# Router fed with unnormalised residual rows, the expert choice taken in two parts, the first-block token table built without counts, and the overflow table moved into the expert turns

## What is computed

```python
h = x + m @ w_out
# channel mixer
xn = rmsnorm(h, norm2_g)
lg = xn @ w_group_router + b_group_router               # 4 groups
grp = argmax(lg); p_grp = softmax(lg)[grp]
le = (xn @ w_expert_router + b_expert_router)[grp]      # 8 experts of that group
top_v, top_i = top_k(le, 2)
wt = p_grp * softmax(top_v); eid = grp * 8 + top_i      # 2 of 32 experts for each row
y = sum over the row's two experts of wt * ((silu(xn @ w_gate[e]) * (xn @ w_up[e])) @ w_down[e])
out = h + y
```

## Time and profile before

| | |
|---|---|
| median of 3 runs | 1861.66 us (1856.81 to 1862.01) |
| the profiled execution's own time | 1863.4 us |
| its span | 1861.6 us |
| PE, DVE, ACT, POOL busy | 93%, 54%, 42%, 17% of the span |
| chain that ended last, by engine | PE 91%, DVE 3%, DMA 3%, ACT 1% |
| TensorE clock granted, mean | 0.96 of full speed |

### The profile page before, as it was taken

One profiled execution on the slowest core, in us unless ns is written; L12 is line 12 of the kernel. 1 busy time (PEld: TensorE's weight loads), 2 busy tenths in 40 slices (PEclk: granted clock), 3 DMA queues, 4 the chain that ended last, 5 costly groups with the idle time before them and its releaser, 6 DMA issues.

```text
span 1861.6 us, 28131 instructions
## 1 busy us (share of the span) xinstructions
PE 1737.7 (93%) x11006; PEld 1560.7 (84%) x11014; DVE 1004.9 (54%) x1392; ACT 774.0 (42%) x1038; POOL 314.6 (17%) x344
## 2 busy tenths in 40 slices
PE   6999999999989999999999899659999999999980
PEld 5999988899979999888899788648888888888870
DVE  5104211277743333212365433359998988989964
ACT  5222211133332223222311222227787878878860
POOL 0001200000101113010101400013333332333310
PEclk9999999999989989999999999769999999999995
DMA  5322432221223223443664322339999999999957
GB/s 183 125 90 83 148 122 78 74 91 64 96 87 110 83 79 109 131 145 118 195 215 129 98 97 87 153 132 379 378 382 380 387 392 392 392 383 383 390 203 292
DMA packets 122881, 365.55 MB, mean 196 GB/s; under 512 B 19089, under 2 KB 79057, under 8 KB 96578
## 3 DMA queue, kind: packets, MB, share of 16 engines
q1 hardware_dynamic: 102210, 312.76, 46.2%
q0 software_dynamic: 19344, 46.99, 6.9%
q10 hardware_dynamic: 1232, 4.46, 0.6%
HBM read 330.41 MB, written 68.52 MB: 214 GB/s over the span
## 4 chain that ended last, share of the span: by engine, by line
PE 91%; DVE 3%; DMA 3%; ACT 1%; issue 1%; POOL 0%; SPq 0%; DVEq 0%; POOLq 0%; ACTq 0%
PE ps L791 15%; PE ps L792 15%; PE ps L793 15%; PE ps L1173 6%; PE ps L1175 6%; PE ps L1174 6%; PE ps L1196 3%; PE ps L1197 3%; PE ps L1198 3%; PE ps L1029 2%; PE ps L966 2%; PE ps L940 2%; PE ps L1162 2%; DMA out_y_prompt<-part 1%; PE ps L1031 1%; PE ps L950 1%
## 5 line engine op out<-in xcount | busy, mean ns | idle before, releaser
L791 PE MATMUL ps<-part,part 128*128 128x256 f32 (+3 forms) x1912 | 609.9, 319 | 11.3 <-DVE part L1783 6.9
L792 PE MATMUL ps<-part,part 128*128 128x256 f32 (+3 forms) x1912 | 595.8, 312 | 0.0
L793 PE MATMUL ps<-part,part 128*128 128x256 f32 (+3 forms) x1912 | 595.6, 311 | 0.0
L1899 DVE TENSOR_TENSOR part<-part,part 128x2048 fp32r<-128x2048 f32 x192 | 440.0, 2293 | 62.0 <-ACT part L1456 57.8
L1456 ACT ACTIVATE part<-part 128x2048 fp32r<-128x2048 f32 x192 | 368.2, 1919 | 116.8 <-PE ps L1175 82.9
L791 PEld LDWEIGHTS ps<-part,part 128*128 128x128 f32 x1912 | 368.2, 193 | 20.1 <-DVE part L1783 8.3
L792 PEld LDWEIGHTS ps<-part,part 128*128 128x128 f32 x1912 | 368.6, 193 | 4.8
L793 PEld LDWEIGHTS ps<-part,part 128*128 128x128 f32 x1912 | 367.7, 192 | 5.1
L1173 PE MATMUL ps<-part,part 128*128 128x512 f32 x512 | 203.8, 398 | 3.5 <-DVE part L1949 3.5
L1175 PE MATMUL ps<-part,part 128*128 128x512 f32 x512 | 200.8, 392 | 0.0
L1174 PE MATMUL ps<-part,part 128*128 128x512 f32 x512 | 200.3, 391 | 0.0
(11 more groups left out here) (229 smaller groups left out, 2017.3 us busy)
## 6 DMA issues: line engine op xcount, KB each, us to landing
part<-w_gate SPq DMA_DIRECT2D x64, 1024.0 KB, 7.8
part<-w_up SPq DMA_DIRECT2D x64, 1024.0 KB, 7.4
part<-w_down SPq DMA_DIRECT2D x64, 1024.0 KB, 7.2
part<-w_in SPq DMA_DIRECT2D x25, 1024.0 KB, 5.4
part<-x_prompt SPq DMA_DIRECT2D x16, 512.0 KB, 3.6
part<-expert_out_scratch SPq DMA_DIRECT2D x8, 1024.0 KB, 6.7
gate_scratch<-part POOLq DMA_DIRECT2D x32, 192.0 KB, 3.0
part<-gate_scratch SPq DMA_DIRECT2D x4, 1088.0 KB, 6.3
```

The lines of the kernel that those rows point to most:

```text
L791: mm(out, lhs[0](k), rhs[0](k), start=(k == 0), stop=False)
L792: mm(out, lhs[0](k), rhs[1](k), start=False, stop=False)
L793: last = mm(out, lhs[1](k), rhs[0](k), start=False, stop=(k == n - 1))
L1899: tt(elo[:, off % NSPL, :], eraw[:, off % NRAW, :], ehi[:, off % NSPL, :].bitcast(F32), ALU.subtract)\
```

## The change

Four things change, and nothing of the expert turns' own work.

1. PE transposes `hbuf`, the rows before normalisation, instead of `x2`. `norm2_g` is multiplied into the router's weights once (`wr` by `g2T`, a sixth load of the router's group, in which each partition gets eight single elements), and the row's reciprocal root is multiplied in when the logits are taken. PE's transposes of a tile stand between the halves of the next tile's matmuls, and its router follows that tile: both one tile sooner than before. On ACT, for the last tile alone, the copy of the transposed rows comes ahead of the root.
2. The choice is made for the first seven tiles of `TORD` (`NEARLY`) ahead of the last tile's sum, and for the other two after the last logits. Ranks count in the order `TORD`.
3. The first-block table needs no counts: the row in the block is the rank itself (a rank of 128 or more matches nothing), the column is the expert. POOL's first three gathers take their indices straight from `tabt`.
4. Counts, overflow bases, slots and the overflow table are made in pieces between expert turns: on PE after turns 2, 4 and 12, on DVE after turns 1, 3 to 11 and 14. The turns up to there are written out, PE's from 2 to 12 and DVE's from 1 to 14. The tokens' weights `wts` (after turn 1) are one of the pieces. `table_ready` 1 is the first-block table, 2 the overflow table, for which only the code after the last turn waits.

```diff
@@ pe @@
-        def x2_transposes(t):
-            pe.wait_ge(s("x2_ready"), t + 1)
+        def h_transposes(i):
+            pe.wait_ge(s("h_ready"), i + 1)
+            if i >= 1:
+                pe.wait_ge(s("hT_ready"), i)
             for k in range(KT):
-                last = tr(pair(4)[:, k, :], x2[t % 2][:, P * k:P * k + P], ident)
+                last = tr(pair(4)[:, k, :], hbuf[:, TORD[i], P * k:P * k + P], ident)
...
+            if i >= 1:
+                out_half(i, 0)
+                h_transposes(i - 1)
+                last = out_half(i, 1)
             last.then_inc(s("out_mm"), 1)
-            if t >= 1:
-                x2_transposes(t - 1)
-            if t >= 2:
-                router(t - 2)
-        router(TILES - 2)
-        x2_transposes(TILES - 1)
+            if i >= 1:
+                router(i - 1)
+        pe.wait_ge(s("assign"), 1)
+        ranks(0, NEARLY)
+        h_transposes(TILES - 1)
         router(TILES - 1)
...
+        pe.wait_ge(s("onehot"), 1)
+        table(0, NEARLY)
+        pe.wait_ge(s("assign"), 2)
+        ranks(NEARLY, TILES)
+        pe.wait_ge(s("onehot"), 2)
+        table(NEARLY, TILES).then_inc(s("tab_mm"), 1)
...
+        OVER_PE = {2: count, 4: block_base, 12: over_table}
...
-        with pe.Fori(2, NE - 1) as b:
+        for b in range(2, 13):
+            gate_up(b, loop_chunks(b), b)
+            x_tr(b + 1)
+            down(b - 1, loop_chunks(b), b)
+            h_tr(b)
+            if b in OVER_PE:
+                OVER_PE[b]()
+        with pe.Fori(13, NE - 1) as b:
@@ dve @@
-            tt(lgt[:, TORD[t], :], bank(6, RW), rbias, ALU.add).then_inc(s("route_in"), 1)
+            stt(lgt[:, i, :], bank(6, RW), small[:, 2, i:i + 1], rbias, ALU.mult, ALU.add).then_inc(s("route_in"), 1)
...
+        def one_hot(t0, t1, part):
+            n = t1 - t0
+            dve.wait_ge(s("rank_mm"), part)
+            ranks = ps[:, 7, NE * t0:NE * t1].rearrange("p (t e) -> p t e", e=NE)
+            for j in range(2):
+                own.done(tt(prank[:, 2 * t0 + j:2 * t1:2, :], E12[:, t0:t1, j, :], ranks, ALU.mult))
+            dve.wait_ge(s("dve_own"), own.n)
+            step(v.tensor_reduce(R["sl"][:, t0:t1, :].rearrange("p t j -> p (t j)"), prank[:, 2 * t0:2 * t1, :], AX.X, ALU.add))
+            tt(in_row[:, 2 * t0:2 * t1, :], cst[:, CIOTA:CIOTA + P].unsqueeze(1).to_broadcast([P, 2 * n, P]),
+               R["sl"][:, t0:t1, :].rearrange("p t j -> p (t j)").unsqueeze(2).to_broadcast([P, 2 * n, P]), ALU.is_equal)\
+                .then_inc(s("onehot"), 1)
...
-        dve.wait_ge(s("rout_in"), 80)
+        dve.wait_ge(s("rout_in"), 96)
+        tt(wr, wr, g2T.unsqueeze(2).to_broadcast([P, KT, RW]), ALU.mult).then_inc(s("wr_ready"), 1)
...
+            if t == TILES - 1:
+                one_hot(0, NEARLY, 1)
...
+            if t == NEARLY:
+                select(0, NEARLY)
+        logits(TILES - 1)
+        select(NEARLY, TILES)
+        one_hot(NEARLY, TILES, 2)
+        dve.wait_ge(s("tab_mm"), 1)
+        step(tsc(tabs[:, 0:NE], ps[:, 2, 0:NE], float(EMPTY), None, ALU.add))
+        tsc(tabt[:, 0:NE], tabs[:, 0:NE], 1, None, ALU.logical_shift_right).then_inc(s("table_ready"), 1)
...
+        OVER_DVE = {1: weights, 3: over_count, 4: over_rank, 5: over_base, 6: over_pos, 7: over_slot, 8: over_where,
+                    9: lambda: over_onehot(0), 10: lambda: (over_onehot(1), over_column()), 11: over_experts, 14: over_tables}
...
-        with dve.Fori(1, NE - 1) as b:
+        for b in range(1, 15):
+            turn(b)
+            if b in OVER_DVE:
+                OVER_DVE[b]()
+        with dve.Fori(15, NE - 1) as b:
             turn(b)
@@ pool @@
-        gather(0, 0)
-        for b in range(1, 3):
-            pool.wait_ge(s("xg_tr"), b)
-            gather(b, b)
+        for b in range(3):
+            if b > 0:
+                pool.wait_ge(s("xg_tr"), b)
+            pool.indirect_dma_start(xg, None, xn_d, bass.IndirectOffsetOnAxis(ap=tabt[:, b:b + 1], axis=0),
+                                    bounds_check=T - 1, oob_is_err=False).then_inc(s("xg_in"), 16)
```

More of the change, by code:

```diff
@@ L100, in constants @@
     c[:, CVALID:CVALID + TILES] = 1
-    c[NSAMP:, CVALID + ST] = 0
+    c[NSAMP:, CVALID + TORD.index(ST)] = 0
     c[:, CEPS] = EPS
@@ L294, in _build @@
     g2b = lh.take(D)
+    g2T = lh.take(KT)
     lh2 = Lay(2 * KT * T + WSLOT)
@@ L298, in _build @@
     x2 = [lh2.take(D) for _ in range(2)]
-    x2T = [lh2.take(KT, P) for _ in range(2)]
+    hTr = [lh2.take(KT, P) for _ in range(2)]
     assert lh2.at <= AFTER_W
@@ L1109, in router, with out_half @@
+        def router(i):
+            pe.wait_ge(s("hT_ready"), i + 1)
+            if i == 0:
+                pe.wait_ge(s("wr_ready"), 1)
+            if i >= 1:
+                pe.wait_ge(s("route_in"), i)
             for k in range(KT):
-                last = mm(bank(6, RW), x2T[t % 2][:, k, :], wr[:, k, :], start=(k == 0), stop=(k == KT - 1))
+                last = mm(bank(6, RW), hTr[i % 2][:, k, :], wr[:, k, :], start=(k == 0), stop=(k == KT - 1))
             last.then_inc(s("rout_mm"), 1)
-        for t in range(TILES):
-            pe.wait_ge(s("m_split"), t + 1)
-            if t >= 2:
-                pe.wait_ge(s("h_ready"), t - 1)
-            if t == 0:
+        def out_half(i, half):
+            return three(bank(2 * (i % 2) + half), [lambda k, v=v: v[i % 2][:, k, :] for v in (mh, ml)],
+                         [lambda k, v=v: v[:, k, 512 * half:512 * half + 512] for v in wo], KT)
@@ new lines, in _, with ranks, table @@
+        ones, before_row = cbf[:, BONE:BONE + P], cbf[:, BLT:BLT + P]
+        def ranks(first, end):
+            for i in range(first, end):
+                out = ps[:, 7, NE * i:NE * i + NE]
+                for i2 in range(i):
+                    mm(out, ones, Abf[:, i2, :], start=(i2 == 0), stop=False)
+                last = mm(out, before_row, Abf[:, i, :], start=(i == 0), stop=True)
+            last.then_inc(s("rank_mm"), 1)
+        def table(first, end):
+            for n in range(2 * first, 2 * end):
+                last = mm(ps[:, 2, 0:NE], in_row[:, n, :], num_col[:, n, :], start=(n == 0), stop=(n == 2 * TILES - 1))
+            return last
@@ L1118, in _ @@
+        for i in range(TILES):
+            pe.wait_ge(s("m_split"), i + 1)
+            if i >= 2:
+                pe.wait_ge(s("h_ready"), i - 1)
+            if i == 0:
                 pe.wait_ge(s("b_gated"), NB_U)
-            for j in range(4 if t == 0 else 0):
+            for j in range(4 if i == 0 else 0):
                 pe.wait_ge(s("w_split"), WO + 1 + j)
@@ L1129, in _ @@
-            if t >= 2:
-                router(t - 2)
-        router(TILES - 2)
-        x2_transposes(TILES - 1)
-        router(TILES - 1)
-        pe.wait_ge(s("assign"), 1)
-        pe.wait_ge(s("route_in"), TILES)
-        ones = cbf[:, BONE:BONE + P]
-        for t in range(TILES):
-            out = ps[:, 0, NE * t:NE * t + NE]
-            order = [ST] + list(range(NTILE))
-            before = order[:order.index(t)]
-            for b4 in before:
-                mm(out, ones, Abf[:, b4, :], start=(b4 == before[0]), stop=False)
-            last = mm(out, cbf[:, BLT:BLT + P], Abf[:, t, :], start=not before, stop=True)
@@ new lines, in over_pos, with over_slot, over_where @@
+        def over_pos():
+            step(tt(pos, pos, R["rank"], ALU.add))
+            step(tt(pos, pos, e128.unsqueeze(1).to_broadcast([P, TILES, NE]), ALU.add))
+        def over_slot():
+            for j in range(2):
+                own.done(tt(prank[:, j:2 * TILES:2, :], E12[:, :, j, :], pos, ALU.mult))
+            dve.wait_ge(s("dve_own"), own.n)
+            step(v.tensor_reduce(R["sl"].rearrange("p t j -> p (t j)"), prank, AX.X, ALU.add))
+        def over_where():
+            step(cp(sloti, R["sl"]))
+            step(tsc(rowi, sloti, P - 1, None, ALU.bitwise_and))
+            step(tsc(blki, sloti, 7, None, ALU.logical_shift_right))
+            step(cp(R["rowf"], rowi))
+            step(cp(R["blkf"], blki))
```

290 lines of the change are left out of this document (148 added, 142 removed).

## The result

| | before | changed |
|---|---|---|
| median | 1863.43 us (8 runs, 1856.81 to 1867.71) | 1848.38 us (8 runs, 1843.45 to 1851.65) |
| ratio | | 0.9919, 95% interval 0.9903 to 0.9935 |
| profiled execution, its span | 1863.4, 1861.6 us | 1851.12, 1849.2 us |

The change is faster by 15.05 us between medians. The two profiled spans differ by 12.4 only, because PE's granted clock dips at different places of the code that both kernels share. So I cut both traces at the same events and add up.

A forecast was written before the change was run, and what follows sets the result against it. PE alone was taken to bound the experts, with a hole ahead of them. The terms -20.75 + 2.4 + 3.1 = -15.25 gave 1848.15 us profiled; the median, 1.7 lower, was forecast at 1846.4 us, range 1840 to 1853.

The forecast's parts named there:

- transposes and router moved ahead: Before the last projection matmul's end: one tile's eight transposes (0.88) and one router (1.87) move ahead, ending it 2.75 us later.
- PE's wait for g2T: At the second tile: PE waits 0.9 us because DVE needs the sixth router load before that tile's remainder.
- the hole: Between the last output-projection matmul and the first gate matmul: shortened so that the first gate matmul starts 20.75 us earlier.
- PE's pieces: In the expert turns: counts 0.3, block bases 0.15 and overflow-table matmuls 1.95 on PE add 2.4 us, bounds 1.5 and 4.5.
- DVE's pieces: In the expert turns: 1.1 us per turn is free on DVE; what exceeds it makes PE wait, 3.1 us in all.
- The bound of 2.1: At the second tile: PE waits 2.1 us if g2T lands after 7.0, as g1T did at the program's start.
- Table to rows: From first-block table to gathered rows: the gather needs no index copy, which saves 3.1 us.
- Weights late next: At the hole's end: DVE's three weight remainders end at 1212.8, after the rows at 1211.8; first gate matmul at 1214.2.
- Rival 1: In the expert turns: DVE's pieces lack cover, 1857.2 us in full, 1851.8 for half; 12 in 100.
- rival 2: Hole and turns: no g2T wait, cheaper PE additions, more cover, full clock sooner (up to 2.1); together 1841.0 us; 11 in 100.
- the plain turns: Sign that the forecast is right: expert turns without a piece take 17.75 us.
- turn 12: Sign that the forecast is right: this expert turn is longer by 2 us.

The follow-up runs named there:

- the probe: The changed kernel with one more DVE step of 1920 elements, its result unused, after each of turns 15 to 30; ratio 1.0021 to the kernel before.

## Why the prediction came out as it did

The forecast was 1846.4 us; 1848.38 was measured, against a median before of 1863.43 where I had 1861.66. The difference, -15.05 between medians and -15.63 in the stretches, stands against a forecast of -15.25. Term by term, though, errors of both signs cancel, and that the sum came so close is luck:

| term | predicted | measured |
|---|---|---|
| transposes and router moved ahead | +2.75 | +2.74 |
| PE's wait for g2T | +0.9 | 0 |
| the hole | -24.4 | -22.64 |
| first expert | 0 | -0.74 |
| PE's pieces | +2.4 | +2.9 |
| DVE's pieces | +3.1 | +2.15 |
| sum | -15.25 | -15.6 |

- **The step that failed** is in the hole: "PE meanwhile transposes the last rows (1 to 2), ACT copies them (1.0), the router takes 3.60 at the low clock, to 1194.7." PE could not do it meanwhile. I had named the PSUM bank's hand-over nowhere, although shows a router waiting for `lgt` (1.96 at 1186.41). The wait of 4.22 us, 3.1 of them beyond ACT's copy, made the ninth logits 2.1 later than forecast; the kernel with the logits first has 4.06 us less, and shows that this was the cause. The low clock that I had put into the router hung on the same wait: without it the router takes 2.10, and the ninth logits would have come 1.9 sooner than forecast.
- **g2T.** DVE went on 3.5 to 5.2 us after its issue in all twelve kernels that have it, not after the 7.0 of the earlier trace rows; in the changed kernel the issue was at 1072.93 and DVE went on at 1078.11. PE waited at the second tile in none of them. The dip of the clock near 1070 us gave all of them extra cover, 1.5 us in the changed kernel, more than the 1.3 that it had to spare there, so its own 0 is no proof. The other eleven had 2.3 to 3.2 us to spare with a dip that cost 1.5 to 1.9, and would not have waited without it. The bound of 2.1 came from a load among larger ones. By the Trainium skill's figure ("DMA: Bandwidth & Descriptors", Bandwidth) I had estimated no wait, and that was right; a landing as short as the 0.7 us of that estimate no run shows.
- **Table to rows**, 3.34 against 3.1 forecast, was right for a reason that I had not seen. The copy is 2.12 long because DVE is busy, and so is the gather's issue. It came out undisturbed only since ACT's exponentials kept DVE's remainders back by 2.2 us (1210.73). The kernel before with this edit alone got 1.87.
- **Weights late next** was right: DVE's third remainder ends at 1217.42, behind ACT's copy of the rows (1215.66 + 1.02), and the stretch behind the transposes is 0.66 longer.
- **DVE's pieces** were mis-sized, 2.15 for 3.1; cover was 1.2 to 1.3, not 1.1, and slots (0.41) and the first half (0.04) cost less than 0.6 and 0.25, counts and base nothing for 0.2 and 0.05. The rule, only what exceeds the cover counts, was confirmed by the probe and by the finer pieces. Rival 1, in full or by half, did not happen.
- **PE's pieces** were 0.5 dearer: counts 0.50 for 0.3 and bases 0.36 for 0.15, too small a price for single small matmuls in a full PE. The overflow table was right, 2.02 for 1.95.
- **The first expert** took 0.74 less, where rival 2 had up to 2.1 for a clock that is up sooner after a shorter hole. That the shorter hole is the cause isn't shown: the kernel before took 13.66 and 13.09 (in the experiment with the index alone), and with the change, without extra matmuls or DVE's wait, it was 12.54 to 12.92 with holes from 26.38 to 36.88, in no order, and 13.24 with the hole of 25.58.

Of the signs that I had named, the weights, the index copy, the plain turns and turn 12 came as said. The first gate matmul came 30.66 after the start of the last projection matmul, outside my 28 to 30, and that one 6.5 later than before and not 3 to 5, 3.57 of it by the clock.

What stays open is what makes the granted clock dip in stretches where PE has no gap. It moved the end of the projection between kernels with the same PE code up to there (1180.20 with all turns written out, 1190.54 with DVE held back; the clock granted up to there makes up 12 us of difference), and it is the scatter in which differences of 2 us drown.

## What to carry to other kernels

Shorten a serial stretch between two full ones by asking of each result what its first reader needs: half of what the hole lost came from a table that no longer waits for counts and a gather that no longer waits for a copy (7.6 and 3.4 us), 6.4 from choosing early for seven tiles, and of the work moved into the turns DVE's 13.1 us cost only 2.15, while PE's cost its full length. Work moved into a stage bound by another engine is free up to a cover that can be read from one turn and costs its full excess beyond that, so cut it to the cover. When a queue of an engine is reordered, list who waits for each instruction that is pushed back, PSUM banks being freed included; that was the 4 us left lying here.

## What the runs showed of the hardware

- A gather's issue on POOL takes 0.99 to 1.08 us with DVE idle at its start, and with a 2048-element DVE step on two SBUF operands under way it ends 0.9 after that step (2.13 to 2.37 at a first gather, 1.89 to 2.99 at 30 of the changed kernel's 32); holding DVE back 2.2 us let PE start 1.39 sooner.
- Bfloat16 matmuls of 512 columns on constants keep the granted clock up through waits: the first expert takes 11.02 instead of 12.92 us. Put where the clock had fallen already, ahead of work that is ready, they cost 2.1.
- The clock falls with PE busy too: 0.66 from 630 to 640 us of the changed kernel, with PE at 10.00 of 10.00 us and no gap ahead of it, against 1.00 at the same place of the kernel before.
- 1512 more matmuls written out (18 turns of 84) make no turn longer, while DMA moves 387 GB/s (1450 to 1750 us of that trace).
